# A decoder trunk whose first feed-forward output run becomes seven block products, in one series with the others

## What is computed

```
def swiglu_ffn(h, w_in, w_out):
    g, u = jnp.split(h @ w_in, [D_FF], axis=-1)
    return (jax.nn.silu(g) * u) @ w_out
...
        yp = yp + swiglu_ffn(rmsnorm(yp, norm_ffn[i]), w_ffn_in[i], w_ffn_out[i])
        ys = ys + swiglu_ffn(rmsnorm(ys, norm_ffn[i]), w_ffn_in[i], w_ffn_out[i])
```

## Time and profile before

| | us |
|---|---|
| median of 3 runs | 1269.87 (1269.87 to 1270.15) |
| the profiled execution's own time | 1270.19 |
| its span, first to last instruction | 1268.4 |
| PE busy | 1244.6 (98%), 9354 matmuls |
| DVE busy | 866.8 (68%) |
| ACT busy | 619.1 (49%) |
| POOL busy | 405.9 (32%) |
| mean granted TensorE clock | 0.997 |

### The profile page before, as it was taken

The page is one execution under the profiler, slowest core; times in us unless marked ns, Lnnn a source line. Parts: engine busy times, 40 slices in busy tenths (PEclk is TensorE's granted clock), DMA queues, the critical chain, the costliest instruction groups (busy, mean ns, idle before and its releaser), DMA issues. The chain is left out here.

```text
span 1268.4 us, 23666 instructions
## 1 busy us (share of the span) xinstructions
PE 1244.6 (98%) x9354; PEld 1199.5 (95%) x9354; DVE 866.8 (68%) x1535; ACT 619.1 (49%) x1158; POOL 405.9 (32%) x255
## 2 busy tenths in 40 slices
PE   9999999999999999999999999999989999999996
PEld 8888899999999999999889998899989999999996
DVE  5776757982287877668447887678962388777655
ACT  5565544562177756743023454224462276766631
POOL 1000034423322222236565544475323322222141
PEclk9999999999999999999999999999999999999998
DMA  9511121272267677733232332223262277777722
GB/s 328 169 35 51 51 66 68 71 165 99 67 161 165 154 170 160 170 107 115 83 101 87 117 125 101 88 70 116 90 142 100 69 165 159 167 162 164 165 84 76
DMA packets 54318, 152.28 MB, mean 120 GB/s; under 512 B 7504, under 2 KB 11536, under 8 KB 52768
## 3 DMA queue, kind: packets, MB, share of 16 engines
q1 hardware_dynamic: 33968, 107.30, 26.3%
q0 software_dynamic: 16704, 30.42, 14.7%
q10 hardware_dynamic: 3536, 13.05, 2.8%
HBM read 143.27 MB, written 9.44 MB: 120 GB/s over the span
## 5 line engine op out<-in xcount | busy, mean ns | idle before, releaser
L684 POOL TENSOR_TENSOR wlo<-wst,whi 128x1024 fp32r<-128x1024 f32 x85 | 212.7, 2502 | 332.9 <-ACT whi L2277 330.2
L728 PE MATMUL ps<-xhi,whi 128*128 128x288 f32 x688 | 209.1, 304 | 1.1 <-DVE wlo L1426 0.7
L729 PE MATMUL ps<-xlo,whi 128*128 128x288 f32 x688 | 202.9, 295 | 0.0
L730 PE MATMUL ps<-xhi,wlo 128*128 128x288 f32 x688 | 202.2, 294 | 0.0
L693 POOL DMA_DIRECT2D wlo<-w_blocks_in x80 | 69.5, 868 | 309.2 <-ACT wlo L2352 297.2
L728 PEld LDWEIGHTS ps<-xhi,whi 128*128 128x128 f32 x688 | 129.0, 187 | 9.6 <-issue 8.3
L728 PE MATMUL ps<-hid,whi 128*128 128x288 f32 x448 | 132.6, 296 | 1.3 <-POOL wlo L684 1.3
L729 PE MATMUL ps<-hid,whi 128*128 128x288 f32 x448 | 132.9, 297 | 0.0
L730 PE MATMUL ps<-hid,wlo 128*128 128x288 f32 x448 | 132.5, 296 | 0.0
L728 PE MATMUL ps<-thi,more_hi 128*128 128x288 f32 x432 | 128.1, 297 | 3.4 <-ACT kept L2361 3.0
L728 PE MATMUL ps<-bhi,whi 128*128 128x288 f32 x432 | 128.1, 297 | 2.6 <-DMA wlo<-w_blocks_in 2.6
(11 more groups left out here) (351 smaller groups left out, 3513.6 us busy)
## 6 DMA issues: line engine op xcount, KB each, us to landing
wst<-w_blocks_in SPq DMA_DIRECT2D x188, 512.0 KB, 3.6
wlo<-w_blocks_in POOLq DMA_DIRECT2D x80, 256.0 KB, 4.2
more_lo<-w_blocks_in POOLq DMA_DIRECT2D x36, 256.0 KB, 6.4
S<-s_in ACTq DMA_DIRECT2D x4, 1024.0 KB, 4.9
s_sample_out<-S ACTq DMA_DIRECT2D x4, 1024.0 KB, 4.6
y_out<-x SPq DMA_DIRECT2D x16, 144.0 KB, 1.9
bias<-bias_in SPq DMA_DIRECT2D x1, 2048.0 KB, 11.5
x<-x_in SPq DMA_DIRECT2D x4, 288.0 KB, 6.7
```

The costliest lines, as they stand in the source:

```text
L684: nc.gpsimd.tensor_tensor(lo, wst[:, slot, :], raw(hi), ALU.subtract).then_inc(w_split, 1)
L728: mm(out, stat[0], mov[0], start=start, stop=False, skip_group_check=skip)
L729: mm(out, stat[0], mov[1], start=False, stop=False, skip_group_check=skip)
L730: return mm(out, stat[1], mov[0], start=False, stop=stop, skip_group_check=skip)
```

## The change

- Output run 0 becomes four seven-product units ("out", 0, i). There is one series, UNITS, of 26 units in each layer: in-4 to in-7, out-0, in-8 ... in-15, out-1, in-16 to in-21. FIRST and LAST are single units.
- Hidden tiles 0 to 7 are kept in halves like 8 to 15: tiles 0 to 3 (direct) are light, tiles 4 to 7 heavy. For the direct tiles up() writes the right half to hT3raw and the left half to h32, half_low() and the T1 sum follow at once, T1 stays raw in early_t1 (the memory of T1's low part), and its high and low parts are made later: early_t1_high in units in-5 and in-6, early_t1_low in in-6 (tiles 0, 1), in-7 (tile 2) and at the start of ("out", 0, 0) (tile 3).
- ScalarE makes S3's high part of a unit after that unit's copy of product 1, not at the end of the unit before. T4's high part moves ahead of S1's.
- In the first output unit of each run: the tile's high part moves ahead of A22; the S2 sum behind the tile's low part and T4's sum; T4's low part ahead of the top sums.
- At the first unit VectorE does the corner sum before tile 3's parts.

The core of the diff:

```diff
-SERIES = ([("in", f) for f in range(N_DIRECT, 8)],
-          [("in", f) for f in TILES[8:16]] + [("out", 1, i) for i in range(4)] + [("in", f) for f in range(16, FC)])
-DOWN_OF = (0, 2)
-UNITS = SERIES[0] + SERIES[1]
-FIRST, LAST = [us[0] for us in SERIES], [us[-1] for us in SERIES]
+UNITS = ([("in", f) for f in range(N_DIRECT, 8)] + [("out", 0, i) for i in range(4)] +
+         [("in", f) for f in TILES[8:16]] + [("out", 1, i) for i in range(4)] + [("in", f) for f in range(16, FC)])
+FIRST, LAST = UNITS[0], UNITS[-1]
...
-    return u is not None and u[0] == "in" and 8 <= u[1] < 16
+    return u is not None and u[0] == "in" and u[1] < 16
...
+        early_t1 = at("hT1early", ht_at["T1"][1], q4)
...
-                    tt(halves(h32), pair(2), halves(gs), ALU.mult).then_inc(u_read[l], 1)
+                    tt(htraw["T3"][:, f, :], ps[:, 3, 0:H], gs[:, H:N], ALU.mult)
+                    tt(h32[:, 0:H], ps[:, 2, 0:H], gs[:, 0:H], ALU.mult).then_inc(u_read[l], 1)
...
+                def early_t1_low(f0, f1):
+
+                    dve.wait_ge(ht_hi["T1"], turn_of(l, f1))
+                    dve.wait_ge(ht_sum["T2"], turn_of(l, f1))
+                    tt(htlo["T1"][:, f0:f1 + 1, :], early_t1[:, f0:f1 + 1, :], raw(hthi["T1"][:, f0:f1 + 1, :]),
+                       ALU.subtract).then_inc(ht_lo["T1"], f1 - f0 + 1)
...
+                def direct_low(f):
+                    half_low(f)
+                    hidden_sum("T1", f)
```

VectorE's loop after the change:

```diff
+                for u, nxt in zip(UNITS, UNITS[1:] + [None]):
...
+                    more, fresh_out = nxt is not None, u[0] == "out" and u[2] == 0
+                    if u == ("out", 0, 0):
+                        early_t1_low(3, 3)
+                    if u == FIRST:
+                        corner(u)
+                        direct_low(3)
+                    elif more:
+                        sum_s1(nxt)
+                    if heavy:
+                        sum_of_hidden_low("T2", f)
+                        sum_of_hidden_low("T3", f)
+                    if prev is not None:
+                        (left_hidden if prev[0] == "in" else left_x)(prev)
+                    if u != FIRST and more and not fresh_out:
+                        sum_s2(nxt)
...
+                    elif prev is not None and prev[0] == "in":
+                        hidden_low(prev[1])
+                    if heavy:
+                        hidden_sum("T4", f)
+                    if fresh_out:
+                        sum_s2(nxt)
+                    if u != FIRST:
+                        if more:
+                            sum_low("S1", nxt)
+                        if fresh_out:
+                            sum_of_hidden_low("T4", f)
+                        top(u)
+                    if more:
+                        sum_s4(nxt)
+                        sum_low("S2", nxt)
...
+                    elif heavy and not fresh_out:
+                        sum_of_hidden_low("T4", f)
+                    if u == ("in", 6):
+                        early_t1_low(0, 1)
+                    if u == ("in", 7):
+                        early_t1_low(2, 2)
+                    if u != FIRST:
+                        corner(u)
+                    if u[0] == "in":
+                        right_hidden(u)
+                    if more:
+                        sum_s3(nxt)
+                        sum_low("S4", nxt)
+                        sum_low("S3", nxt)
+                    prev = u
```

ScalarE's:

```diff
+                for u, nxt in zip(UNITS, UNITS[1:] + [None]):
...
+                    copy(1, u)
+                    if u != FIRST:
+                        quarter_high("S3", u)
+                    if heavy:
+                        sum_high("T2", f)
+                        sum_high("T3", f)
+                    if nxt is not None:
+                        quarter_high("A11", nxt)
...
+                    copy(5, u)
...
+                    if u[0] == "out" and u[2] == 0:
+                        hidden_high(f)
                         quarter_high("A22", u)
...
+                    copy(6, u)
+                    if heavy:
+                        sum_high("T4", f)
+                    if nxt is not None:
+                        quarter_high("S1", nxt)
+                    if light:
+                        sum_high("T1", f)
+                    if nxt is not None:
+                        quarter_high("S2", nxt)
+                        quarter_high("A12", nxt)
+                    if u == ("in", 5):
+                        early_t1_high(0, 1)
+                    if u == ("in", 6):
+                        early_t1_high(2, 3)
+                    if u[0] == "in":
+                        silu(u[1])
+                    if nxt is not None:
+                        quarter_high("S4", nxt)
```

More of the change, by code:

```diff
@@ L74 @@
 TILES = (list(range(8)) + [8 + 4 * (i % 2) + i // 2 for i in range(8)] + list(range(16, FC)))
-WHOLE_TILES = [f for f in TILES if not 8 <= f < 12]
+WHOLE_TILES = [f for f in TILES if f >= 16 or f % 8 >= 4]
 def block_order():
@@ L121, in by_transfer @@
 def by_transfer(q, u):
-    return u not in FIRST and not (q == "A22" and u in LAST)
+    return u != FIRST and (q, u) != ("A22", LAST)
 def transfers(q, l, u):
@@ L537, in quarter_free @@
         def quarter_free(eng, q, l, u):
-            if q not in ("S1", "S2", "A22") and u in FIRST:
+            if q not in ("S1", "S2", "A22") and u == FIRST:
                 eng.wait_ge(*used(blocks_of(l, u)[0] - (2 if q in ("A11", "A12") else 1)))
@@ L700, in ffn @@
                     split(n)
[L701 to L709, removed]
+                quarter_low("A11", l, FIRST)
+                quarter_low("A12", l, FIRST)
+                for u, nxt in zip(UNITS, UNITS[1:]):
+                    quarter_low("A11", l, nxt)
+                    quarter_low("A22", l, u)
+                    quarter_low("A12", l, nxt)
+                for n in DOWN_AT[l][2]:
+                    split(n)
             nc.gpsimd.memset(zero[:, :], 0.0).then_inc(zeroed, 1)
@@ L1015, in product @@
                     for c in range(4):
[L1016 to L1019, removed]
+                        if u[0] == "out" and u[2] == 0:
+                            f = 8 * u[1] + c
+                            if op in ("B21", "B22"):
+                                pe.wait_ge(h_lo[l], whole_tiles(f + 4))
+                            else:
+                                pe.wait_ge(b_lo if op == "B11" else ht_lo[op], turn_of(l, f))
                         w = slice(c * P, (c + 1) * P)
@@ L1035, in seven @@
                     o, a = ordinal(l, u), bank_of(u)
-                    last, fresh_out = u in LAST, u == ("out", 1, 0)
+                    last, fresh_out = u == LAST, u[0] == "out" and u[2] == 0
                     if o > 2:
@@ L1081, in down @@
                         ins.then_inc(w_used, 1)
-                for ph, us in zip(DOWN_OF, SERIES):
-                    before = None
-                    for u in us:
-                        seven(u, before)
-                        before = u
-                    n_in = PHASES[ph][1] - PHASES[ph][0]
-                    down(ph, 0, 0, 2)
-                    left_up(before)
-                    down(ph, 0, 2, n_in)
-                    for m in range(1, KC - 2 if l and ph else KC):
-                        down(ph, m, 0, n_in)
+                before = None
+                for u in UNITS:
+                    seven(u, before)
+                    before = u
+                n_in = PHASES[2][1] - PHASES[2][0]
+                down(0, 0, 2)
+                left_up(before)
+                down(0, 2, n_in)
+                for m in range(1, KC - 2 * l):
+                    down(m, 0, n_in)
                 if l:
@@ L1590, in hidden_sum @@
                     out, left, right = htraw[op][:, j, :], h32[:, 0:H], h32[:, H:N]
-                    if op == "T1":
+                    if op == "T1" and f < N_DIRECT:
+                        dve.wait_ge(u_read[l], f + 1)
+                        out, a, b = early_t1[:, j, :], htraw["T3"][:, j, :], left
+                    elif op == "T1":
                         dve.wait_ge(seven_read, ordinal(l, ("in", f)))
@@ L1613, in h32_read @@
                 def h32_read(f):
-                    if 8 <= f < 12:
+                    if f < 16 and first_half(f):
                         dve.wait_ge(b_lo, turn_of(l, f))
@@ L1867, in _ @@
+                left_hidden(prev)
+                hidden_low(prev[1])
+                if l == 0:
+                    dve.wait_ge(h_lo[0], len(WHOLE_TILES))
+                    nc.vector.memset(raw(shi[:, :, :]), 0.0)
+                    ins = nc.vector.memset(raw(slo[:, :, :]), 0.0)
+                    chain.link(ins)
+                for m in range(KC - 2 * l):
+                    down(m)
             ffn(0)
```

230 lines of the change are left out of this document (75 added, 155 removed).

## The result

| | before | after |
|---|---|---|
| median of 10 runs, us | 1270.12 (1269.2 to 1271.23) | 1275.35 (1272.96 to 1279.11) |
| profiled execution, span | 1270.19, 1268.4 | 1279.11, 1277.3 |
| matmuls | 9354 | 9258 |
| mean granted clock | 0.997 | 0.991 |

The ratio is 1.0043, with a 95% interval of 1.0035 to 1.005: 5.2 us slower. The forecast was 1268.5 with a range up to 1273.5, so it missed by 6.9 us and the range missed too. The profiled execution is the slowest of the ten; it is 10.3 us above its own forecast of 1268.4 - 1.4 = 1267.0 for the span. The ten runs spread over 6 us, where those of before spread over 2.

What follows compares the result with a forecast made beforehand. TensorE's own matmul work was taken as the bound. The terms -12.8 + (9.6 + 0.4 - 2.2) + (9.6 + 0.4 - 4.0) - 2.4 = -1.4 us took the median 1269.87 to 1268.5, range 1261.5 to 1273.5.

Steps and rivals of the forecast that it cites:

- 96 fewer matmuls: First output run on TensorE: four units of 84 replace 384 plain matmuls, 48 fewer a layer, 12.8 us saved in all.
- The ring: VectorE and ScalarE hand-overs in units in-5 to in-7: 12.15 us a turn against TensorE's 11.2, stalls 9.6 a layer.
- The gap: First output unit's second product, waiting for T1's low part: 4 to 5 of the 9.6 us stalls, in one piece.
- Copies ahead of sums: At the first unit the copy comes some 1.3 us sooner, but the hand-overs take it back: worth nothing.
- The later output run: Shorter waits for tile 15's low part (1.2), corner sums (0.7) and A22 with similar ones (0.5): 2.4 us gained.
- Other output units: Those after the first output unit were to run like today's four, with no wait.
- rival 3: A late A11 transfer in layer 1 after the fuller output run, one or two more, +1 to +2 each: 1271; chance 0.07.
- The clock left at 1.00 in the sum: The forecast sum for the whole kernel held no cost for TensorE's clock falling behind the first output unit's gap.
- the rival: The first output unit's gap drops TensorE's clock, 3.2 us each: 1271.7 in one layer, 1274.9 in both; chance 0.18.

Runs made afterwards that it cites:

- run 0: Not a follow-up run: the first output run in each layer, plain products of 384 matmuls before the change, four units of 84 after; no separate time given.
- S3 before the copy: The changed kernel with ScalarE making S3's high part at the end of the unit before, ahead of copy 1: 1275.7 us.
- the filled gap: The changed kernel with 24 useless matmuls in TensorE's queue ahead of the wait for tile 3's T1: 1270.57 us, ratio 1.0005 to the kernel before.
- the last kernel: Changed kernel, T4's high part later in input units, tile 3's T1 low part earlier, product 4 ahead of 5, A11 ahead of S3 in output units: 1259.71 us.
- T1 early: The changed kernel with tile 3's low part of T1 made on VectorE at the end of in-7, ahead of S3's sum: 1268.68 us.
- product 4 first: The changed kernel with product 4 of in-7 done ahead of the first output unit's product that waits for T1: 1269.54 us.
- A11 sooner: The changed kernel with A11 of the next unit made on ScalarE ahead of S3 in the second output unit of each run: 1270.97 us.
- the load later: The changed kernel with SyncE's second block load held until the accumulating transfer of A11 has landed: 1271.73 us.

## Why the prediction was wrong

- **96 fewer matmuls, 12.8 us.** Right: 9258 against 9354.
- **The ring, 12.15 us a turn.** Right. The first corner sum stood at 260.03 (forecast 260.0), the S3 sums at 263.76 (263.8) and 301.16 (301.3), the gap ended at 303.72 (303.8). Stalls up to there: 303.72 - 248.52 - 345 x 0.133 = 9.3 in layer 0 and 9.6 in layer 1 (913.03 to 968.51), forecast 9.6.
- **The gap, "4 to 5 us".** 3.84, a little under; the rest came as small stalls.
- **Copies ahead of sums, nothing in total.** Right, as the kernel with S3 before the copy shows, though each side of that balance was larger than thought.
- **The later output run, 2.4 us.** The waits that were to go went, and were worth 2.9 (tile 15's low part 1.9 to 0.2, corners 1.2 to below the list; in gaps from start to start 1.23, 1.24, 1.06 and 0.72 became 0.49, none, 0.36 and 0.35). But 2.8 us was taken back by late A11 transfers: gaps of 1.18 and 0.93 at the third unit of both layers and 1.04 at the first unit of layer 1, each less 0.13. The run gained 0.1.
- **"Other output units: the same as the four of today, no wait."** This step failed: 4.1 us in the first run and 2.8 in the later one. I took the transfer's 4.2 us from the median of the earlier trace rows and let it stand for a new order of issues. In the output run of before the load behind the transfer was as near (1.12 us), but the load ahead landed sooner (1.10 us behind the issue). In the third output units of the changed kernel, with the load ahead landing 2.14 to 3.93 behind the issue, it took 6.1 to 7.5. Taking the second load away, or moving the transfer ahead of S3, takes the gap of the first run away; why the order of the changed kernel brings the three transfers together just there was not followed. My rival 3 had the mechanism, a late A11, but the wrong place and weight: behind the first output run, +1 to +2 at 0.07, and as an alternative to the sum.
- **The clock left at 1.00 in the sum.** This step failed too, and it is the larger part: 6.0 us in the profile, 4.8 by the filled gap. I had the rival, with its price (3.2 a fall; 2.7 and 1.6 measured for the two behind the long gap, with matmuls 0.24 apart where I had put 0.27), and gave it 0.18. The forecast was of a gap longer than any that a feed-forward layer had, and the only row on what follows one, spoke for a fall. My argument against it, that the stall might come in pieces, spoke against my own number of 4 to 5 us "as one gap". The rule of the Trainium skill ("TensorE: Matmul & The Clock Gate", Part 1: The HAM clock gate), that idleness puts the throttle back, was the right one, in the middle of a dense kernel too. The trace agrees, with 0.50 at 303.00 to 309.80.

The two failed steps were rivals with prices, each taken as an alternative to the sum. The fall was a consequence of the forecast itself, and the two add: 1268.5 + 4.8 + 4.4 - 1.4 for what they share = 1276.3, against 1275.35. (The three numbers behind 1268.5 come from the runs, so this says again that 1267.57, the time without the two, is 0.9 from the forecast.)

## What to carry over

A gap that you forecast as one piece has a second price: look in the trace for what the clock did behind a gap of that length, and put it into the sum, not beside it. A median of a transfer's time is read under the old order of issues; when a stretch is rebuilt, ask for each transfer that is waited for what else is in flight beside it, the load ahead as well as the load behind, and look whether it can be issued apart from them. And shortening a ring that drives an engine does not shorten the gap at its end if it brings that engine there sooner as well; that needs a move inside the last stretch.

## What the runs showed of the hardware

- Gaps between starts of 3.84, 3.26 and 3.52 us were each followed by a stretch at 0.50, in every profile that has them; so were 2.78 and 2.63 with S3 before the copy, 2.29 and 2.09 at transfers, 2.06 in the last kernel, A11 sooner in all output units (296.42), and 1.79 in layer 1 with T1 early. Gaps of 1.79 in layer 0 of the same kernel, 1.99 before, 1.92 and 1.88 with product 4 first, 2.06 in the changed kernel (326.25) and 2.46 in the last (953.41) were not. So between 1.8 and 2.5 us the length alone does not tell. Where a fall came, it lasted 3.4 us, or 6.8 in some profiles (layer 0 of the changed kernel; both layers with A11 sooner; layer 1 with the load later), for the same gap of 3.84.
- This may be what makes the time spread: 1272.96 to 1279.11 after, 1269.2 to 1271.23 before. Each run at 1.2 GHz loses 1.6 to 2.7 us. That the spread is these falls was not shown: the kernel with the gap filled, with no fall in its profile, still ran from 1268.27 to 1272.74; the mean clock of the ten runs is 0.990 to 0.993 and does not follow their times closely.
- An accumulating transfer of 256 KB took 4.0 to 4.7 us in 17 places of the changed kernel with a 512 KB load issued 1.1 us behind it, and 6.1 to 7.5 in the four where the load ahead of it also landed over 2 us behind its issue (as it did in one of the 17). With the load 1.64 us behind it took 4.62 and 4.65 in the first output run and 5.55 and 5.67 in the later one. What decides inside the queues stays open.
